# Filler multiplications on TensorE between the last modulation pieces and the first normalized tile

## The reference, cut to what matters

```python
cs = jax.nn.silu(c)
for i in range(DEPTH):
    mod = (cs @ ada_w[i] + ada_b[i])[:, None, :]
    sh1, sc1, g1, sh2, sc2, g2 = jnp.split(mod, 6, axis=-1)
    h = rms_norm(x, norm1_g[i]) * (1.0 + sc1) + sh1
    ...
            mix = dilated_attention(h, attn_w_in[j], attn_w_out[j])   # proj = h @ w_in first
    x = x + g1 * mix
    h = rms_norm(x, norm2_g[i]) * (1.0 + sc2) + sh2
    x = x + g2 * conv_ffn(h, ...)
```

## Time and profile before

| | |
|---|---|
| median of 3 executions | 2772.11 us (2771.10 to 2777.31) |
| span of the profiled execution, first to last instruction | 2774.0 us |
| TensorE busy | 2705.1 us, 98% |
| VectorE busy | 2261.5 us, 82% |
| mean granted clock | 0.988 |

### The profile page before, as it was taken

How to read it: one execution, slowest core, us unless ns; L and a number is a source line. 1 busy time by engine, 2 the same in 40 slices (tenths; PEclk the granted TensorE clock), 3 DMA queues, 4 the chain that set the end, 5 groups by cost and what they waited for, 6 DMA issues and landing times.

```text
span 2774.0 us, 55516 instructions
## 1 busy us (share of the span) xinstructions
PE 2705.1 (98%) x21388; PEld 2480.4 (89%) x21388; DVE 2261.5 (82%) x3001; ACT 1263.1 (46%) x1775; POOL 489.5 (18%) x461
## 2 busy tenths in 40 slices
PE   5999999999999999999999999999999999999998
PEld 1998888888899999999999999999788888888887
DVE  6978878777789888889889988998898975677755
ACT  2444444444434444434444344444365543455542
POOL 4142110101132000000110331244311100011122
PEclk8999999999999999999999999999999999999999
DMA  9989877877766888878888967778777766555563
GB/s 375 386 265 332 319 273 266 279 264 268 243 219 211 322 300 302 280 239 321 328 301 308 369 225 247 233 257 321 260 241 239 256 180 188 191 187 184 182 186 109
DMA packets 241846, 724.67 MB, mean 261 GB/s; under 512 B 51056, under 2 KB 60016, under 8 KB 240880
## 3 DMA queue, kind: packets, MB, share of 16 engines
q1 hardware_dynamic: 185184, 666.98, 69.2%
q10 hardware_dynamic: 56464, 54.95, 6.3%
HBM read 700.60 MB, written 25.43 MB: 262 GB/s over the span
## 4 chain that ended last, share of the span: by engine, by line
PE 85%; DVE 4%; issue 1%; POOL 1%; DMA 1%; ACT 0%; ACTq 0%; DVEq 0%; POOLq 0%
PE proj L1872 30%; PE proj L1875 14%; PE proj L1877 12%; PE proj L1878 11%; PE proj L1879 11%; DVE w_lo L1146 1%; PE proj L1871 1%; DVE acc L1052 1%; PE ps L1993 1%; PE ps L2083 1%; DVE work L1452 0%; PE pmisc L1902 0%; PE pturn L2110 0%; PE ps L2110 0%; PE ps L1991 0%
## 5 line engine op out<-in xcount | busy, mean ns | idle before, releaser
L590 ACT ACTIVATE w_hi<-raw 128x1024 fp32r<-128x1024 f32 (+1 forms) x896 | 934.2, 1043 | 1067.6 <-PE proj L1879 429.1
L1146 DVE TENSOR_TENSOR w_lo<-raw,w_hi 128x1024 fp32r<-128x1024 f32 (+1 forms) x896 | 1106.9, 1238 | 335.3 <-ACT w_hi L590 332.5
L1872 PE MATMUL proj<-h_hl,w_hi 128*128 128x512 f32 x3008 | 1057.0, 399 | 3.3 <-DVE h_hl L1100 2.3
L1875 PE MATMUL proj<-h_hl,w_lo 128*128 128x256 f32 x2820 | 791.2, 281 | 0.0
L1872 PEld LDWEIGHTS proj<-h_hl,w_hi 128*128 128x128 f32 x3008 | 555.4, 188 | 125.3 <-DVE h_hl L1100 2.5
L1877 PE MATMUL proj<-h_hl,w_hi 128*128 128x256 f32 x2112 | 610.0, 289 | 10.8 <-DVE h_hl L1100 6.3
L1878 PE MATMUL proj<-h_hl,w_hi 128*128 128x256 f32 x2112 | 601.8, 285 | 0.0
L1879 PE MATMUL proj<-h_hl,w_lo 128*128 128x256 f32 x2112 | 601.6, 285 | 0.0
L1875 PEld LDWEIGHTS proj<-h_hl,w_lo 128*128 128x128 f32 x2820 | 532.9, 189 | 7.1
L1877 PEld LDWEIGHTS proj<-h_hl,w_hi 128*128 128x128 f32 x2112 | 408.1, 193 | 16.8 <-issue 9.3
L1878 PEld LDWEIGHTS proj<-h_hl,w_hi 128*128 128x128 f32 x2112 | 409.3, 194 | 0.0
(11 more groups left out here) (261 smaller groups left out, 2371.1 us busy)
## 6 DMA issues: line engine op xcount, KB each, us to landing
ada<-in_ada_w SPq DMA_DIRECT2D x352, 512.0 KB, 5.6
raw<-in_w_up SPq DMA_DIRECT2D x352, 512.0 KB, 5.1
raw<-in_w_in SPq DMA_DIRECT2D x224, 512.0 KB, 5.4
raw<-in_w_down SPq DMA_DIRECT2D x128, 448.0 KB, 3.9
raw<-in_w_down SPq DMA_DIRECT2D x64, 512.0 KB, 4.1
raw<-in_w_out SPq DMA_DIRECT2D x32, 512.0 KB, 4.8
raw<-in_ssm_w_in SPq DMA_DIRECT2D x32, 512.0 KB, 4.8
raw<-in_ssm_w_gate SPq DMA_DIRECT2D x32, 512.0 KB, 5.7
```

The lines of the kernel that those rows point to most:

```text
L590: nc.scalar.activation(w_hi[:, j % LAG, 0:nk * P], raw[:, j % s.ring, 0:nk * P], ACT.Copy).then_inc(hi_ready, 1)
L1146: V.tensor_tensor(w_lo[:, j % LAG, 0:nk * P], raw[:, j % s.ring, 0:nk * P], w_hi[:, j % LAG, 0:nk * P].bitcast(F32), ALU.subtract).then_in ...
L1872: ins = mm(both, w_hi[:, j % LAG, w], hl[:, k].rearrange("p c t -> p (c t)"), start=(k == 0), stop=end)
L1875: ins = mm(o, w_lo[:, j % LAG, w], hi[:, k, :], start=False, stop=False)
```

## The change

A function `keep_busy(n)` is added on TensorE's queue. It waits for x, on whose arrival the squares at line 582 waited too, and issues n matmuls of 128 x 128 by 128 x 128 float32 tiles of x into `ps0`. Nothing reads what they write. It is called behind pieces 28, 29 and 30 with 2, 2 and 6 matmuls, and behind `spread_root(0)` with 6: 16 matmuls. No other engine's instructions change.

```diff
+            def keep_busy(n):
+
+                pe.wait_ge(x_in, 16)
+                for k in range(n):
+                    mm(ps0[:, 0:P], x[:, k, 0:P], x[:, k + 1, 0:P], start=True, stop=True)
+
             pe.wait_ge(cs_ready, 1)
             for n in range(2 * KT):
...
                 ins.then_inc(ada_summed, 1)
+                if n >= 28:
+                    keep_busy((2, 2, 6, 0)[n - 28])
             spread_root(0)
+            keep_busy(6)
             pe.wait_ge(ones_ready, 1)
             pe.wait_ge(lam_copied, 1)
```

## The result

| | median us | lowest to highest | executions |
|---|---|---|---|
| before | 2772.48 | 2769.00 to 2777.47 | 20 |
| changed | 2776.95 | 2771.69 to 2782.07 | 20 |

Ratio 1.0013, 95% interval 1.0007 to 1.0019: slower, by 3.7 us in the means (2776.61 against 2772.92). The median lies outside the range given, 2768.5 to 2776.0 us, and on the other side of before than forecast. Over all 53 executions that the changed kernel had in the end, its mean is 2775.8 us.

The account below looks back on a forecast made before the run. The prediction took DVE and transfers to set the pace from 60 to about 130 us, hanging on piece 31's end. Terms -0.44 + 0 + 0 us from the median 2772.11 gave 2771.7 us, range 2768.5 to 2776.0 us.

Parts of the forecast that it names:

- What bounds the start: From 60 to about 130 us DVE and transfers set the pace; the end of piece 31 decides, TensorE has slack.
- Part 1: Fillers between pieces 28 and 31: clock rises before piece 31, releasing DVE and SP 0.44 us earlier; bounds -0.44 and +0.57 us.
- sign of being wrong: Listed signs include piece 31 starting later than its transfer, and w_lo of piece 3 earlier by more than 0.5 us.
- upper bound of the term: Fillers between pieces 28 and 31, clock low throughout: piece 31 starts and everything behind comes 0.57 us later.
- Part 2: Six fillers behind `spread_root`: 1.3 us at the high clock or 2.6 us at the low, at no cost to the total.
- part 3: Products of pieces 0 and 1 at the higher clock: 1.58 us of TensorE saved, all absorbed waiting for piece 3's w_lo.
- The sum: Whole kernel: -0.44 us from piece 31, 0 from fillers behind the root, 0 from products; 2771.7 us, 0.02% faster.
- The noise case: Rival called "Something between", chance 0.05: low stretches at later norms shift between executions, changing the time 1 to 2 us either way.
- The late rise: Rival, chance 0.33: clock does not rise before piece 31, which ends 0.1 to 0.57 us late; 2772.2 to 2772.7 us.
- The passed-on clock: Rival, chance 0.05: DVE and transfers follow TensorE, so the regained clock reaches the end; 2765.6 us, faster by 0.23%.
- The slower one: Rival, chance 0.03: longer wait ahead of piece 3, then a long low clock stretch behind 79 us; 2778.3 us.
- Within 0.2%: Outcome class for the whole kernel's time: less than 0.2% (5.5 us) from before, given a chance of 0.91.

Follow-up runs that it names:

- one-column fillers: The change with its 16 fillers streaming one column in place of 128, against the kernel before: pooled mean 2777.14 us, +4.4 +-0.6 us.
- displaced kernels: Kernels with TensorE's code moved by 6, 10, 16 or 48 matmuls, against code in place or moved by 64: state-space stretch 18.1 against 16.9 us in the mean.
- padded change: The change with 48 small matmuls added at the start of TensorE's program, against the kernel before: pooled mean 2773.95 us, +1.3 +-0.4 us.

## Why the prediction was wrong

**What bounds the start** was right in the main. DVE's chain hangs on piece 31, and the time that the products gain by the clock is waited away: 1.81 us ahead of piece 2 and 0.34 us ahead of piece 3, where before had 1.94 us ahead of piece 3. The prediction had no wait ahead of piece 2.

**Part 1** was right about the clock and too high in size. The clock rose before piece 31 in all four traces of the change, and its group took 0.64 us. Set against the earlier trace rows it ended 0.5 us earlier (0.44 forecast), but that agreement is luck: the earlier trace rows is one of five traces of this start, which end piece 31 between 59.16 and 60.51 us, and in the means the gain is 0.1 us, which is nothing beside that scatter. The term took the start of piece 31 as unmoved; its fillers were mis-sized, so that piece 31 follows them without a wait in three traces of four, which the prediction itself had listed as a sign of being wrong. A filler takes 0.26 us at the high level (six from 57.41 to 58.95 us), where I had 0.22, and 0.58 us at the low (two from 53.96 to 55.12 us), where I had 0.43; a piece at the low level holds TensorE for 1.01 us, where I had 0.85. The upper bound of the term was too low for the same reason: with the one-column fillers, where the clock stayed low, piece 31 began 1.3 us late and not 0.57.

**Part 2 and part 3** held: the six fillers behind the root end at 61.6 us, the first product starts at 62.84 us. w_lo of piece 3 came at 78.12 us, forecast 78.7, and at 78.12 to 78.91 us over the four traces. It is over 0.5 us earlier than in the earlier trace rows, which was to be a sign of being wrong; the five traces of the same start, 77.3 to 79.3 us, show that a single pair can't decide that. The wait that I expected in one piece of 3.5 us ahead of piece 3 fell apart into two of together 2.15 us, and piece 2 ran at the low clock for 3.4 us (1.7 us of work), which took the rest.

**The sum** failed, by what it left out. It has a term for the time that the fillers take and one for the clock, and sets everything behind 130 us to zero. It named no term for where the instructions behind them lie. The runs put +2.3 +-0.4 us on that, for 16 matmuls that take no time, and 1.8 +-0.5 us for it in the change, from what 48 small matmuls at the start take off. The traces give two places for it: +0.8 us between 190 and 270 us, much the same in every trace, and 1.5 us in the mean of four, with a scatter of 2 us, at the start of the state-space layer. The remaining 1.3 +-0.4 us of the padded change is not told apart from what 48 small matmuls alone cost (+1.0 +-0.6): of the forecast gain of 0.44 us nothing can be seen, and of a loss by the fillers as such nothing certain either.

**The noise case** ("Something between") named the right place and the wrong behaviour. I took low stretches at the later norms as falling either way from one execution to the next, so that they leave the mean alone. The start of the state-space layer, which I did not list among them, is such a place too, and there the traces of the displaced kernels lean to one side: a low stretch falls there in eight of thirteen, against one of seven for the others.

**The rivals.** The late rise is out, since the clock rose before piece 31 in all four traces; what it priced, a piece 31 held up by the fillers, happened in part all the same. The passed-on clock is out by the waits. The slower one was priced by a low stretch behind 79 us, and that did not happen (3.4 us at most, as before). The Trainium skill's penalty (TensorE: Matmul & The Clock Gate, section Terms) would have credited the change with half of the low clock that it removed; the kernel lost 3.1 us with a higher mean clock (0.990 against 0.989 over the timed executions). **The range** reached 4.3 us above the forecast; it rested on the scatter of three executions and had no systematic term in it. **Within 0.2%**, to which I gave 0.91, is where it ended.

What stays open: how the place of TensorE's code lengthens a wait that depends on transfers and other engines. That an instruction transfer falls into the read of `u_d` in the kernels displaced by 16 and not in before is seen; that it delays the read was not tried by itself, and two traces speak against it as the whole cause. A rule by the place within a block fits the transfers and the times of 16 and 64, but not the stretch from 190 to 270 us, where 48 and 64 alike gain 0.7 us; that 48 matmuls ahead help by something other than filling the block is not excluded. Where the padded change loses its 1.3 us its two traces do not show: they are short in both places. Nor do I know why the one-column fillers lose 1.3 +-0.7 us more than the change without the padding and nothing more with it.

## What to carry to other kernels

An edit that adds instructions to one engine moves all later code of that engine, and that can cost several times the edit's own time, or in single stretches gain (+0.8 and -0.7 us in one of them here): time the edit beside a twin that adds the same number of instructions where they cost nothing, and one that adds none ahead of the rest. For effects of 0.1% compare means of dozens of executions and time the kernel against itself first. A faster clock under a stage that is paced by another engine turns into waiting, which the wait ahead of the next stage shows in advance. A gain of half a microsecond read off one pair of traces is not a gain until the unchanged program has been traced several times: here its own traces of that spot lay 1.4 us apart.

## What the runs showed of the hardware

Instructions are themselves transferred while the kernel runs, in packets of 16 KB that hold some 256 of TensorE's instructions (20 of them while 2537 matmuls and as many weight loads ran): adding 256 added one packet (136 to 137), adding 64 or 192 none. Sixteen small matmuls, which occupy TensorE for less than 1 us, cost 1.7 to 3.5 us wherever they stood ahead of the state-space layer and nothing at the end of the program (0.0 +-0.7); 64 of them at the start cost 0.0 +-0.6. The stretch from 190 to 270 us took 70.6 us with nothing added, 71.4 us behind 6 to 16 more matmuls and 69.9 us behind 48 or 64. At the low clock a float32 matmul with 128 columns of weights takes 0.48 us for one column of data (two from 53.74 to 54.69 us) and 0.58 us for 128; one with two columns of weights and one of data takes 0.05 us (64 in 3.34 us). The clock's low stretches at the norms fell at other moments, and lasted 6.8 or 10.2 us, in different traces of one and the same program.
